# GpSimd takes the low halves of the gate weights and the splitting of each head's output; a head's sink becomes one more column of its scores

## The chip, the cores and the metric

The kernel runs on one NeuronCore of a Trainium2 chip. Five engines work from instruction queues of their own, each in order, and meet only at semaphores: TensorE (PE in the profile, with its weight loads shown apart as PEld), VectorE (DVE), ScalarE (ACT), GpSimd (POOL) and SyncE (SP), which here issues most DMA transfers. The metric is the device time of one execution in microseconds; the median of three runs stands for the kernel.

## The reference

A trunk of two layers over 512 tokens of width 1024, float32. What matters here is the mixer block of each layer:

```python
def mixer_block(h, w_in, b_gate, rel_bias, sinks, w_branch_a, w_branch_b, w_out):
    proj = h @ w_in        # q, k, v of both attentions, and 2048 gate columns
    ya = chunk_relpos_attention(qa, ka, va, rel_bias)      # 8 heads of 64, all earlier chunks
    yb = swa_sink_alibi_attention(qb, kb, vb, sinks)       # 8 heads of 64, 2 chunks back at most
    gates = jax.nn.sigmoid(gate_logits + b_gate)
    merged = gates[:, :, 0] * (ya @ w_branch_a) + gates[:, :, 1] * (yb @ w_branch_b)
    return merged @ w_out

# inside swa_sink_alibi_attention, per head:
    scores = einsum(q, k) * d ** -0.5 + alibi
    m = jnp.maximum(jnp.max(scores, axis=-1, keepdims=True), sink)
    e = jnp.exp(scores - m)
    probs = e / (jnp.sum(e, axis=-1, keepdims=True) + jnp.exp(sink - m))
```

So the sink is a learned number per head that takes part in a row's maximum and in its sum, and has no value vector. Layer 0 ends in a dense SwiGLU, layer 1 in a top-2-of-8 expert SwiGLU.

## The kernel before, in words

Every float32 product is made of three products of rounded halves: a value x is split into hi = round(x) and lo = x - hi, both of a 32-bit type that TensorE takes in one pass, and hi·hi + lo·hi + hi·lo is summed in PSUM. Weights come by DMA in units of 128x1024 into `raw` (4 buffers); ScalarE copies a unit to `w_hi` (`split_hi`), VectorE subtracts to get `w_lo` (`split_lo`, L890), and TensorE multiplies (L1273 to L1275). `w_hi` and `w_lo` have 2 buffers, so unit n+2 is split while unit n+1 is multiplied.

The change lies in the attention stage, which each layer runs through once. It is a loop of 64 steps, called ticks, 4 for each of 16 heads (one for each 128 query rows). Ticks 0 to 31 are heads of kind A, whose rows see 128, 256, 384 and 512 keys; ticks 32 to 63 are heads of kind B, which see 128 or 256 keys. Each engine's program is written out by hand in the order of ticks, and steps of different age are interleaved. In tick t:

- TensorE transposes the probabilities of step t-2 (L1411, after a wait for `probs_ready`), makes the scores of step t (L1421, L1422), multiplies older probabilities by the values (L1439, L1440), and between them works through a quarter of a gate unit (`gate_part`: 6 large products, L1273 to L1275), so that a head has one gate unit beside it. For A heads it also turns the next head's bias (L1384).
- VectorE adds the bias to the scores and takes the negated row maximum in one instruction (L993, in PSUM; in kind B the sink is its starting value), then takes the reciprocal of the sum of step t-1 (L1005) and scales its probabilities by it in SBUF (L1007); in kind B the exponential of the sink is first added to the sum (L1002). Then it makes the low half of the transposed probabilities of step t-2 (L893, `pT_lo`).
- ScalarE copies the high half of the transposed probabilities (L704), and exponentiates the scores (L714); in kind B the sink before them (L712).
- Once per head, in the head's first tick (tick % 4 == 0): ScalarE makes `w_hi` of a gate unit (L595) and then `y_other`, half of an older head's output (L732). VectorE scales a gate's result (L923), makes `w_lo` (L890) and adds the two halves of the output into `y_sum` (L1027), which waits for `y_other`. In the next tick ScalarE copies `y_sum` to its high half (L738) and VectorE subtracts to get the low half (L893, `q_both<-y_sum`). ScalarE also writes the next head's bias tile: out of the turned bias in kind A (L620), as a scaled copy of a distance table in kind B (L623).
- GpSimd has one piece of work per A head: it fetches the next head's bias by DMA (L476) and clears a corner of it (L479). In the 32 ticks of kind B it has none.

After tick 67 the branch products begin (w_a and w_b), which wait for the low half of the last head (`y_lo_ready`).

Of the kernel before, what the change touches and what calls it, by code (L numbers as in the profile page):

```python
# [5 lines left out]
F32 = mybir.dt.float32  # L6
# [8 lines left out]
P = 128  # L15
D = 1024
T = 512
# [46 lines left out]
def build_kernel(nc, xT, g_mix, w_in, b_gate, rel_ext, sinks, w_a, w_b, w_out, g_ffn, w_gu, w_down, w_router,  # L64
                 moe_gu, moe_down, g_ffn_row, g_final_row, out):
    ctx = ExitStack()
    with ctx:
        def sb(name, shape, dt=F32, where=ctx):
            return where.enter_context(nc.sbuf_tensor(name, shape, dt))
# [49 lines left out]
        bias_t = sb("bias_t", [P, 2, T], F32, attn)  # L119
# [6 lines left out]
        nsink = sb("nsink", [P, DEPTH, HEADS], F32, attn)  # L126
# [88 lines left out]
        sink_exp, exp_ready, denom, rcp_ready, probs_ready = sem("sink_exp"), sem("exp_ready"), sem("denom"), sem("rcp_ready"), sem("probs_ready")  # L215
# [219 lines left out]
        def _(pool):  # L435
# [33 lines left out]

            for i in range(DEPTH * HEADS):  # L470
# [117 lines left out]
        def _(act_):  # L588
# [25 lines left out]

            def bias_tile(H, bank):

                layer, hh = H // (2 * HEADS), H % (2 * HEADS)
                if hh < HEADS:
                    A.wait_ge(bias_turned, layer * HEADS + hh + 1)
                    A.activation(bias_t[:, H % 2, 2 * P:], ps[:, bank, 2 * P:], ACT.Identity,  # L620
                                 bias=nfar[:, layer, hh:hh + 1]).then_inc(bias_ready, 1)
                else:
                    A.activation(bias_t[:, H % 2, 2 * P:], alibi[:], ACT.Copy,  # L623
                                 scale=-2.0 ** -(step(TT * hh)["head"] + 1)).then_inc(bias_ready, 1)
# [36 lines left out]
            for layer in range(DEPTH):  # L661
# [33 lines left out]
                for tick in range(STEPS + 6):  # L695
                    if 2 <= tick < STEPS + 2:
                        s, st = layer * STEPS + tick - 2, step(tick - 2)
                        A.wait_ge(pT_ready, s + 1)
                        if st["qb"] == 0 and st["hh"] < 2 * HEADS - 1:
                            bias_tile(layer * 2 * HEADS + st["hh"] + 1, T_BANK + s % 2)  # L700
                        if s >= 4:

                            A.wait_ge(pv_done, s // 2 - 1)
                        A.activation(pT_hi[:, own_blocks(tick - 2), :],  # L704
                                     ps[:, T_BANK + s % 2, 0:st["nk"]].rearrange("p (b c) -> p b c", c=P),
                                     ACT.Copy).then_inc(pT_hi_ready, 1)
                    if tick < STEPS:
                        s, st = layer * STEPS + tick, step(tick)
                        A.wait_ge(nmax_ready, s + 1)
                        c = s % 4  # L710
                        if not st["a"]:
                            A.activation(stat[:, 3, c:c + 1], sink[:, layer, st["head"]:st["head"] + 1], ACT.Exp,  # L712
                                         bias=stat[:, 1, c:c + 1]).then_inc(sink_exp, 1)
                        A.activation(probs[:, s % 2, 0:st["nk"]], ps[:, S_BANK + s % 2, 0:st["nk"]], ACT.Exp, scale=-1.0,  # L714
                                     bias=stat[:, 1, c:c + 1], accum_out=stat[:, 2, c:c + 1]).then_inc(exp_ready, 1)
# [17 lines left out]
                    if tick >= 9 and tick % 4 == 1:  # L733
                        hh = (tick - 9) // 4
                        H = layer * 2 * HEADS + hh
                        r = step(4 * hh)["rows"]
# [149 lines left out]
        def _(V):  # L886
# [38 lines left out]
            def small_consts():  # L925
                V.wait_ge(small_in, 16 * N_SMALL)
                V.tensor_scalar(bg[:], bg[:], 0.5, None, ALU.mult)
                V.tensor_scalar(nfar[:], far[:], -1.0, None, ALU.mult)
                V.tensor_scalar(nsink[:], sink[:], -1.0, None, ALU.mult).then_inc(consts, 1)
# [14 lines left out]
            for layer in range(DEPTH):  # L944
# [39 lines left out]
                for tick in range(STEPS + 6):  # L984
                    if tick < STEPS:
# [4 lines left out]
                        if st["qb"] == 0:  # L990
                            V.wait_ge(bias_ready, H + 1)

                        V.tensor_tensor_reduce(out=sc[:, 0:nk], in0=sc[:, 0:nk], in1=bias_t[:, H % 2, T - nk:], scale=-1.0,  # L993
                                               scalar=-MASKED if st["a"] else nsink[:, layer, st["head"]:st["head"] + 1],
                                               op0=ALU.add, op1=ALU.min, accum_out=stat[:, 1, c:c + 1]).then_inc(nmax_ready, 1)
                    if 1 <= tick < STEPS + 1:
# [3 lines left out]
                        den = stat[:, 2, c:c + 1]  # L1000
                        if not st["a"]:
                            V.tensor_tensor(stat[:, 4, c:c + 1], den, stat[:, 3, c:c + 1], ALU.add).then_inc(denom, 1)  # L1002
                            V.wait_ge(denom, layer * STEPS // 2 + tick - STEPS // 2)
                            den = stat[:, 4, c:c + 1]
                        V.reciprocal(stat[:, 5, c:c + 1], den).then_inc(rcp_ready, 1)  # L1005
# [9 lines left out]
                    if (tick - 4) in GATES_AT:  # L1015
# [4 lines left out]
                        split_lo(n + 2)  # L1020
                    if tick >= 8 and tick % 4 == 0:
# [4 lines left out]
                        V.wait_ge(y_moved, H + 1)  # L1026
                        V.tensor_tensor(y_sum[r:r + HD, :], ps[r:r + HD, O_BANK + hh % 2, :], y_other[r:r + HD, :],  # L1027
                                        ALU.add).then_inc(y_added, 1)
                    if tick >= 9 and tick % 4 == 1:
                        hh = (tick - 9) // 4  # L1030
                        r = step(4 * hh)["rows"]
                        y_hi, y_lo = y_tiles(hh)
                        V.wait_ge(y_hi_ready, layer * 2 * HEADS + hh + 1)
                        lo_of(y_lo[r:r + HD, :], y_sum[r:r + HD, :], y_hi[r:r + HD, :]).then_inc(y_lo_ready, 1)

                for i in range(N_BR // 2):
                    n = n0 + U_BR + 2 * i
                    split_lo(n + 2)
# [227 lines left out]
        def _(E):  # L1266
# [73 lines left out]
            for layer in range(DEPTH):  # L1340
# [46 lines left out]
                for tick in range(STEPS + 4):  # L1387
# [25 lines left out]
                    if tick < STEPS:  # L1413
                        s, st = layer * STEPS + tick, step(tick)
                        k0, nk, qb = st["k0"], st["nk"], st["qb"]
                        if s >= 2:
                            E.wait_ge(exp_ready, s - 1)
                        out = ps[:, S_BANK + s % 2, 0:nk]
# [267 lines left out]
```

## Time and profile before

| | us |
|---|---|
| median of 3 runs (lowest, highest) | 1753.32 (1751.65, 1756.61) |
| span of the profiled execution, first to last instruction | 1750.1 |
| attention loop of layer 0, scores of tick 0 to last products with values | 121 to 296.7 |
| attention loop of layer 1 | 867 to 1041.6 |
| PE busy | 1611.9 (92%) |
| DVE busy | 1097.2 (63%) |
| ACT busy | 884.1 (51%) |
| POOL busy | 99.2 (6%) |

The profile is one execution, and its span leaves out what lies between the start of the measured time and the first instruction. The chain of work that ended last runs 76% over PE, 12% over DVE and 5% over ACT. Matmuls are pipelined and overlap in the records, so PE is never quite at its peak where it is busy.

### The profile page before, as it was taken

The page shows a single profiled execution, that of the slowest core. Times are in us where ns is not written, and L with a number is a line of the kernel's source. Part 1 is how long each engine was busy: PE and PEld are TensorE (multiplying, and loading weights), DVE is VectorE, ACT ScalarE, POOL GpSimd, SP SyncE. Part 2 cuts the span into 40 slices and gives each one's busy share as a digit, 9 for nine tenths or more (in the row PEclk, how much of TensorE's full clock was granted, in tenths as well). Part 3 has the DMA queues.
Part 4 walks back from the last instruction along what each step waited for, and adds up shares of the span by engine and source line. Part 5 has one row for each costly group of instructions (what it writes and reads, how often), then busy time and mean ns, then how long its engine had stood idle before and what let it go on. Part 6 is the DMA issues. An engine that isn't in the chain of part 4 may idle for free.

```text
span 1750.1 us, 22696 instructions
## 1 busy us (share of the span) xinstructions
PE 1611.9 (92%) x7630; PEld 1328.5 (76%) x7631; DVE 1097.2 (63%) x1794; ACT 884.1 (51%) x1422; POOL 99.2 (6%) x148
## 2 busy tenths in 40 slices
PE   8999987999999999999999879969999999999991
PEld 5877765878888878888777658747888888888880
DVE  6647876654444433346478765565656988876665
ACT  5436665243333322234366652445556888875653
POOL 2000000000000000010000000040000001110101
PEclk9999998999999999999999999989999999999995
DMA  7332111223333323343321112155767999997764
GB/s 200 112 96 61 52 49 49 85 84 96 96 97 97 96 81 97 100 134 110 102 61 52 49 48 84 49 229 159 237 200 239 358 364 365 362 338 224 221 221 175
DMA packets 79109, 259.46 MB, mean 148 GB/s; under 512 B 12384, under 2 KB 12384, under 8 KB 78512
## 3 DMA queue, kind: packets, MB, share of 16 engines
q1 hardware_dynamic: 71056, 239.16, 41.6%
q0 software_dynamic: 7968, 19.21, 3.9%
q8 instruction: 48, 0.79, 0.2%
q14 instruction: 37, 0.30, 0.1%
HBM read 244.70 MB, written 9.47 MB: 145 GB/s over the span
## 4 chain that ended last, share of the span: by engine, by line
PE 76%; DVE 12%; ACT 5%; DMA 3%; issue 3%; POOL 0%; SPq 0%; ACTq 0%; POOLq 0%; DVEq 0%; PEldq 0%
PE ps L1273 15%; PE ps L1275 15%; PE ps L1274 15%; PE ps L1553 6%; PE ps L1555 6%; PE ps L1554 6%; PE ps L1551 3%; PE ps L1552 3%; DVE w_lo L890 2%; DVE ps L993 2%; ACT w_hi L595 1%; PE ps L1411 1%; DVE y_sum L1027 1%; DVE m_lo L1175 1%; PE ps L1534 1%
## 5 line engine op out<-in xcount | busy, mean ns | idle before, releaser
L1175 DVE TENSOR_TENSOR m_lo<-m_raw,m_hi 128x1024 fp32r<-128x1024 f32 (+1 forms) x285 | 324.4, 1161 | 110.5 <-ACT m_hi L800 106.7
L800 ACT ACTIVATE m_hi<-m_raw 128x1024 fp32r<-128x1024 f32 (+1 forms) x285 | 284.0, 1010 | 167.8 <-PE ps L1552 132.2
L1273 PE MATMUL ps<-h_hi,w_hi 128*128 128x512 f32 x904 | 361.9, 400 | 5.8 <-DVE h_lo L909 2.9
L595 ACT ACTIVATE w_hi<-raw 128x1024 fp32r<-128x1024 f32 (+1 forms) x169 | 177.1, 1048 | 367.9 <-PE ps L1275 364.6
L1274 PE MATMUL ps<-h_lo,w_hi 128*128 128x512 f32 x904 | 354.5, 392 | 0.0
L1275 PE MATMUL ps<-h_hi,w_lo 128*128 128x512 f32 x904 | 354.4, 392 | 0.0
L890 DVE TENSOR_TENSOR w_lo<-raw,w_hi 128x1024 fp32r<-128x1024 f32 (+1 forms) x169 | 204.7, 1211 | 188.7 <-ACT w_hi L595 186.8
L1275 PEld LDWEIGHTS ps<-h_hi,w_lo 128*128 128x128 f32 x904 | 170.4, 189 | 36.9
L1273 PEld LDWEIGHTS ps<-h_hi,w_hi 128*128 128x128 f32 x904 | 170.9, 189 | 34.3 <-DVE w_lo L890 5.0
L1274 PEld LDWEIGHTS ps<-h_lo,w_hi 128*128 128x128 f32 x904 | 171.0, 189 | 26.7 <-issue 0.7
L1553 PE MATMUL ps<-m_hi,xt_hi 128*128 128x512 f32 (+1 forms) x384 | 145.5, 379 | 6.3 <-DVE m_lo L1175 5.0
L1555 PE MATMUL ps<-m_hi,xt_lo 128*128 128x512 f32 (+1 forms) x384 | 143.5, 374 | 0.0
L1554 PE MATMUL ps<-m_lo,xt_hi 128*128 128x512 f32 (+1 forms) x384 | 143.4, 373 | 0.0
L1553 PEld LDWEIGHTS ps<-m_hi,xt_hi 128*128 128x128 f32 x384 | 72.8, 190 | 19.6 <-DVE m_lo L1175 5.2
L1411 PE MATMUL ps<-ident,probs 128*128 128x128 f32 x272 | 52.8, 280 | 31.9 <-DVE probs L1007 31.7
L714 ACT ACTIVATE probs<-ps,stat 128x256 f32<-128x256 f32 (+3 forms) x128 | 61.2, 478 | 41.3 <-DVE stat L993 40.2
L1554 PEld LDWEIGHTS ps<-m_lo,xt_hi 128*128 128x128 f32 x384 | 72.8, 190 | 10.2
L1555 PEld LDWEIGHTS ps<-m_hi,xt_lo 128*128 128x128 f32 x384 | 72.5, 189 | 10.2
L1411 PEld LDWEIGHTS ps<-ident,probs 128*128 128x128 f32 x272 | 34.7, 140 | 59.2 <-DVE probs L1007 49.3
L1552 PE MATMUL ps<-m_lo,xt_both 128*128 128x512 f32 (+1 forms) x192 | 72.2, 376 | 0.0
L1551 PE MATMUL ps<-m_hi,xt_both 128*128 128x512 f32 (+1 forms) x192 | 72.2, 376 | 0.0
L1553 PE MATMUL ps<-m_hi,at_hi 128*128 128x512 f32 x176 | 70.7, 402 | 1.6 <-PEq L1567 1.6
(234 smaller groups left out, 2759.5 us busy)
## 6 DMA issues: line engine op xcount, KB each, us to landing
m_raw<-moe_g SPq DMA_DIRECT2D x135, 512.0 KB, 5.1
m_raw<-moe_down SPq DMA_DIRECT2D x88, 512.0 KB, 5.2
raw<-w_in SPq DMA_DIRECT2D x68, 512.0 KB, 3.5
m_raw<-moe_g SPq DMA_DIRECT2D x64, 384.0 KB, 3.8
raw<-w_gu SPq DMA_DIRECT2D x44, 512.0 KB, 3.5
raw<-w_out SPq DMA_DIRECT2D x16, 512.0 KB, 3.5
raw<-w_down SPq DMA_DIRECT2D x16, 512.0 KB, 3.6
raw<-w_a SPq DMA_DIRECT2D x8, 512.0 KB, 3.4
```

The lines of the kernel that those rows point to most:

```text
L595: A.activation(split_of(n, 0, cols)[0], raw[:, n % RAW, 0:cols], ACT.Copy).then_inc(hi_ready, 1)
L800: A.activation(m_hi[:, u % M_SPL, 0:cols], m_raw[:, u % M_RAW, 0:cols], ACT.Copy).then_inc(m_hi_ready, 1)
L890: V.tensor_tensor(lo, raw[:, n % RAW, 0:cols], hi.bitcast(F32), ALU.subtract).then_inc(lo_ready, 1)
L1175: V.tensor_tensor(m_lo[:, u % M_SPL, 0:cols], m_raw[:, u % M_RAW, 0:cols], m_hi[:, u % M_SPL, 0:cols].bitcast(F32), ALU.subtract).then_inc ...
L1273: E.matmul(ps[:, bank, :], wh, hi, start=first, stop=False)
L1274: E.matmul(ps[:, bank, :], wh, lo, start=False, stop=False)
L1275: return E.matmul(ps[:, bank, :], wl, hi, start=False, stop=final)
L1551: E.matmul(out, both[:, x, :], wh, start=start, stop=False)
L1552: return E.matmul(out, both[:, x, :], wl, start=False, stop=stop)
L1553: E.matmul(out, hi[:, x, :], wh, start=start, stop=False)
L1554: E.matmul(out, hi[:, x, :], wl, start=False, stop=False)
L1555: return E.matmul(out, lo[:, x, :], wh, start=False, stop=stop)
```

## The change

GpSimd does three things more in the attention stage: `w_lo` of the 16 gate-stage units of each layer (`gate_lo`), both halves of each head's output (`head_split`), and the bias tile of each B head (`distance_tile`), with the head's sink in a 513th column. VectorE and ScalarE lose these. In kind B the sink is now one more column of the scores: VectorE's instruction takes one more PSUM column, which is zero, adds the bias tile with the sink in it, and writes its sum not to PSUM but to `probs` in SBUF; ScalarE exponentiates there, in place, one column more, and its running sum holds the sink's part already. The separate exponential, the addition to the sum and the negated sinks are gone. TensorE's wait before the scores of step t is for the maximum of step t-2 in kind B, not for its exponential.

The new functions of GpSimd, the order in which it calls them, and what goes from VectorE and ScalarE:

```diff
+            def gate_lo(layer, g):
+                n = MIX_START[layer] + U_GATE + g + 2
+                hi, lo = split_of(n, 0, UNIT)
+                pool.wait_ge(hi_ready, n + 1)
+                pool.wait_ge(lo_ready, n)
+                pool.tensor_tensor(lo, raw[:, n % RAW, :], hi.bitcast(F32), ALU.subtract).then_inc(lo_ready, 1)
+                pool.wait_ge(lo_ready, n + 1)
+            def distance_tile(layer, hh):
...
+                pool.wait_ge(nmax_ready, TT * (H - 1))
+                pool.tensor_scalar(bias_t[:, H % 2, 2 * P:T], alibi[:], -2.0 ** -(head + 1), None, ALU.mult)
+                pool.wait_ge(bias_ready, H)
+                pool.tensor_copy(bias_t[:, H % 2, T:T + 1], sink[:, layer, head:head + 1]).then_inc(bias_ready, 1)
+            def head_split(layer, hh):
...
+                pool.wait_ge(y_added, H + 1)
+                pool.tensor_copy(y_hi[r:r + HD, :], y_sum[r:r + HD, :]).then_inc(y_hi_ready, 1)
+                pool.wait_ge(y_hi_ready, H + 1)
+                pool.tensor_tensor(y_lo[r:r + HD, :], y_sum[r:r + HD, :], y_hi[r:r + HD, :].bitcast(F32),
+                                   ALU.subtract).then_inc(y_lo_ready, 1)
+                pool.wait_ge(y_lo_ready, H + 1)
             for i in range(DEPTH * HEADS):
...
+                pool.wait_ge(bias_masked, i + 1)
+                if i % HEADS >= 2:
+                    gate_lo(i // HEADS, i % HEADS - 2)
+                if i % HEADS >= 3:
+                    head_split(i // HEADS, i % HEADS - 3)
+                if i % HEADS == HEADS - 1:
+                    for j in range(HEADS - 2, 2 * HEADS):
+                        gate_lo(i // HEADS, j)
+                        head_split(i // HEADS, j - 1)
+                        if j + 2 < 2 * HEADS:
+                            distance_tile(i // HEADS, j + 2)
+                    head_split(i // HEADS, 2 * HEADS - 1)
...
-                        if not st["a"]:
-                            A.activation(stat[:, 3, c:c + 1], sink[:, layer, st["head"]:st["head"] + 1], ACT.Exp,
-                                         bias=stat[:, 1, c:c + 1]).then_inc(sink_exp, 1)
+                            A.activation(probs[:, s % 2, 0:st["nk"] + 1], probs[:, s % 2, 0:st["nk"] + 1], ACT.Exp, scale=-1.0,
+                                         bias=stat[:, 1, c:c + 1], accum_out=stat[:, 2, c:c + 1]).then_inc(exp_ready, 1)
...
-                        A.wait_ge(y_added, H + 1)
-                        A.activation(y_tiles(hh)[0][r:r + HD, :], y_sum[r:r + HD, :], ACT.Copy).then_inc(y_hi_ready, 1)
...
+                            if tick < STEPS // 2 + 2:
+                                V.memset(sc[:, 2 * P:2 * P + 1], 0.0).then_inc(sink_column, 1)
+                                V.wait_ge(sink_column, 2 * layer + tick - STEPS // 2 + 1)
+                            V.wait_ge(pT_ready, s - 1)
+                            V.tensor_tensor_reduce(out=probs[:, s % 2, 0:nk + 1], in0=sc[:, 2 * P - nk:2 * P + 1],
+                                                   in1=bias_t[:, H % 2, T - nk:T + 1], scale=-1.0, scalar=-MASKED,
+                                                   op0=ALU.add, op1=ALU.min, accum_out=stat[:, 1, c:c + 1]).then_inc(nmax_ready, 1)
...
-                            V.tensor_tensor(stat[:, 4, c:c + 1], den, stat[:, 3, c:c + 1], ALU.add).then_inc(denom, 1)
...
-                        split_lo(n + 2)
...
-                        lo_of(y_lo[r:r + HD, :], y_sum[r:r + HD, :], y_hi[r:r + HD, :]).then_inc(y_lo_ready, 1)
```

On VectorE, in the middle of a B head of the program before, from the last row of the head's first tick to the first rows of the third (`w_lo` is the gate weights' low half, `q_both<-y_sum` the head's):

```order
L923 TENSOR_TENSOR gates<-ps,rms_inv 128x512
L890 TENSOR_TENSOR w_lo<-raw,w_hi 128x1024
L1027 TENSOR_TENSOR y_sum<-ps,y_other 64x512
L993 ISA ps,stat<-ps,bias_t,nsink 128x256
L993 ISA stat 128x1
L1002 TENSOR_TENSOR stat<-stat 128x1
L1005 RECIPROCAL stat<-stat 128x1
L1007 TENSOR_SCALAR probs<-probs,stat 128x128
L893 TENSOR_TENSOR pT_lo<-ps,pT_hi 128x2x128
L893 TENSOR_TENSOR q_both<-y_sum,q_both 64x512
L993 ISA ps,stat<-ps,bias_t,nsink 128x256
```

The same place in the changed program (L1034 is now the addition with the maximum, L1043 the scaling):

```order
L956 TENSOR_TENSOR gates<-ps,rms_inv 128x512
L1064 TENSOR_TENSOR y_sum<-ps,y_other 64x512
L1034 ISA probs,stat<-ps,bias_t 128x257
L1034 ISA stat 128x1
L1041 RECIPROCAL stat<-stat 128x1
L1043 TENSOR_SCALAR probs<-probs,stat 128x128
L926 TENSOR_TENSOR pT_lo<-ps,pT_hi 128x2x128
L1034 ISA probs,stat<-ps,bias_t 128x257
```

Three instructions are gone from between the gate's scaling and the next step's scores, two of them large. On GpSimd, for the last A heads before, where it goes from bias to bias:

```order
L479 MEMSET norm 64x64
L476 DMA norm<-rel_ext 128x256
L479 MEMSET norm 64x64
L476 DMA norm<-rel_ext 128x256
```

and in the changed program, through the last of these biases into the first of the B heads:

```order
L507 DMA norm<-rel_ext 128x256
L510 MEMSET norm 64x64
L475 TENSOR_TENSOR w_lo<-raw,w_hi 128x1024
L495 CAST q_both<-y_sum 64x512
L497 TENSOR_TENSOR q_both<-y_sum,q_both 64x512
L475 TENSOR_TENSOR w_lo<-raw,w_hi 128x1024
L495 CAST q_both<-y_sum 64x512
L497 TENSOR_TENSOR q_both<-y_sum,q_both 64x512
L485 TENSOR_SCALAR bias_t<-alibi 128x256
L487 COPY bias_t<-sink 128x1
```

Each head now gives GpSimd a weight unit and an output in two instructions, and in kind B a bias tile, all in one queue.

## Rows read from the trace of the kernel before

**Rows 1.** Windows, kind A and kind B ticks: us, busy per engine, PEclk, DMA, GB/s.
```profile
121.20:205.20 84.00, 79.36 (x432) 65.09 (x430) 61.91 (x182) 54.88 (x130) 5.03 (x14) 0.98 0.21 60
205.20:289.10 83.90, 69.03 (x385) 54.58 (x383) 66.66 (x217) 55.99 (x163) 0.00 (x0) 1.00 0.17 51
```

**Rows 2.** Timeline of a B head's long tick: start us, us, engine, line, instruction [idle before].
```profile
238.62 1.05 ACT L595 ACTIVATE w_hi<-raw 128x1024 fp32r<-128x1024 f32 x1
...
239.70 0.59 ACT L732 ACTIVATE y_other<-ps 64x512 f32<-64x512 f32 x1
239.71 1.23 DVE L890 TENSOR_TENSOR w_lo<-raw,w_hi 128x1024 fp32r<-128x1024 f32 x1
...
240.96 0.69 DVE L1027 TENSOR_TENSOR y_sum<-ps,y_other 64x512 f32<-64x512 f32 x1
...
242.59 0.29 DVE L1007 TENSOR_SCALAR probs<-probs,stat 128x128 f32<-128x128 f32 x1
...
242.93 0.33 PE L1411 MATMUL ps<-ident,probs 128*128 128x128 f32 x1 [1.59 <-DVE probs L1007]
```

**Rows 3.** Timeline, TensorE's last score product (L1422) of each tick, two B heads.
```profile
226.87 0.28 PE L1422 MATMUL ps<-kb_lo,q_both 128*128 128x128 f32 x1
...
237.32 0.28 PE L1422 MATMUL ps<-kb_lo,q_both 128*128 128x128 f32 x1
239.44 0.28 PE L1422 MATMUL ps<-kb_lo,q_both 128*128 128x256 f32 x1
243.22 0.29 PE L1422 MATMUL ps<-kb_lo,q_both 128*128 128x256 f32 x1
...
248.42 0.28 PE L1422 MATMUL ps<-kb_lo,q_both 128*128 128x128 f32 x1
```

**Rows 4.** Groups by form: count | busy us, mean ns of one | idle before, releaser.
```profile
L893 DVE TENSOR_TENSOR q_both<-y_sum,q_both 64x512 fp32r<-64x512 f32 x32 | 22.0, 686 | 12.6 <-ACT q_both L738 12.6
L738 ACT ACTIVATE q_both<-y_sum 64x512 fp32r<-64x512 f32 x32 | 20.0, 624 | 3.6 <-DVE y_sum L1027 3.2
L712 ACT ACTIVATE stat<-sink,stat 128x1 f32<-128x1 f32 x64 | 18.8, 294 | 44.8 <-DVE stat L993 44.5
L1007 DVE TENSOR_SCALAR probs<-probs,stat 128x512 f32<-128x512 f32 x16 | 7.8, 487 | 0.7
```

**Rows 5.** Groups of GpSimd by form.
```profile
L516 POOL TENSOR_TENSOR h_rows<-h_rows,g_row 128x1024 f32<-128x1024 f32 x4 | 9.4, 2354 | 8.3 <-ACT h_rows L631 8.2
L479 POOL MEMSET norm<- 64x64 f32 x16 | 2.5, 158 | 45.1 <-DMA norm<-rel_ext 45.1
L519 POOL MEMSET m_act<- 64x512 f32 x1 | 0.5, 517 | 0.0
```

**Rows 6.** Timeline of the kernel's last stage, where VectorE and GpSimd work beside each other.
```profile
1735.06 1.28 DVE L1254 SCALAR_TENSOR_TENSOR x_rows<-h_rows,r,x_rows 128x1024 f32<-128x1024 f32 x1
1736.06 2.49 POOL L584 TENSOR_TENSOR x_rows<-x_rows,g_row 128x1024 f32<-128x1024 f32 x1 [17.02 <-ACT x_rows L882]
1736.33 3.30 DVE L1251 SCALAR_TENSOR_TENSOR x_rows<-h_rows,r,x_rows 128x1024 f32<-128x1024 f32 x1
```

**Rows 7.** Timeline, a clearing by GpSimd that begins beside a scaling.
```profile
129.92 0.42 DVE L1007 TENSOR_SCALAR probs<-probs,stat 128x384 f32<-128x384 f32 x1
130.08 0.35 POOL L479 MEMSET norm<- 64x64 f32 x1 [2.69 <-DMA norm<-rel_ext]
```

**Rows 8.** Timeline of two A heads: weight split and the next tick's scaling.
```profile
152.46 1.05 ACT L595 ACTIVATE w_hi<-raw 128x1024 fp32r<-128x1024 f32 x1
...
156.22 0.29 DVE L1007 TENSOR_SCALAR probs<-probs,stat 128x128 f32<-128x128 f32 x1
...
163.38 1.05 ACT L595 ACTIVATE w_hi<-raw 128x1024 fp32r<-128x1024 f32 x1
...
166.78 0.28 DVE L1007 TENSOR_SCALAR probs<-probs,stat 128x128 f32<-128x128 f32 x1
```

**Rows 9.** Timeline, the first branch product after the attention loop of layer 0.
```profile
299.53 0.79 PE L1273 MATMUL ps<-q_both,w_hi 128*128 128x512 f32 x1 [2.79 <-DVE q_both L893]
```

More of the change, by code:

```diff
@@ L468, in double_keys @@
                         pool.dma_start(lo[other, :], lo[own, :]).then_inc(k_doubled, 16)
+            def gate_lo(layer, g):
[6 more added lines that the diff above has]
+            def distance_tile(layer, hh):
+                H = layer * 2 * HEADS + hh
+                head = step(TT * hh)["head"]
+                if hh == HEADS:
+                    pool.wait_ge(consts, 4)
+                pool.wait_ge(nmax_ready, TT * (H - 1))
[3 more added lines that the diff above has]
+            def head_split(layer, hh):
+                H = layer * 2 * HEADS + hh
+                r = step(4 * hh)["rows"]
+                y_hi, y_lo = y_tiles(hh)
+                pool.wait_ge(y_added, H + 1)
[4 more added lines that the diff above has]
+                pool.wait_ge(y_lo_ready, H + 1)
             for i in range(DEPTH * HEADS):
@@ L617, in bias_tile @@
                 layer, hh = H // (2 * HEADS), H % (2 * HEADS)
[L618 to L624, printed above, removed]
+                A.wait_ge(bias_turned, layer * HEADS + hh + 1)
+                A.activation(bias_t[:, H % 2, 2 * P:T], ps[:, bank, 2 * P:], ACT.Identity,
+                             bias=nfar[:, layer, hh:hh + 1]).then_inc(bias_ready, 1)
             def x_copy(t):
@@ L927, in small_consts @@
                 V.tensor_scalar(bg[:], bg[:], 0.5, None, ALU.mult)
-                V.tensor_scalar(nfar[:], far[:], -1.0, None, ALU.mult)
-                V.tensor_scalar(nsink[:], sink[:], -1.0, None, ALU.mult).then_inc(consts, 1)
+                V.tensor_scalar(nfar[:], far[:], -1.0, None, ALU.mult).then_inc(consts, 1)
                 V.wait_ge(consts, 3)
@@ L999, in _ @@
                         V.wait_ge(exp_ready, s + 1)
-                        den = stat[:, 2, c:c + 1]
-                        if not st["a"]:
-                            V.tensor_tensor(stat[:, 4, c:c + 1], den, stat[:, 3, c:c + 1], ALU.add).then_inc(denom, 1)
-                            V.wait_ge(denom, layer * STEPS // 2 + tick - STEPS // 2)
-                            den = stat[:, 4, c:c + 1]
-                        V.reciprocal(stat[:, 5, c:c + 1], den).then_inc(rcp_ready, 1)
+                        V.reciprocal(stat[:, 5, c:c + 1], stat[:, 2, c:c + 1]).then_inc(rcp_ready, 1)
                         V.wait_ge(rcp_ready, s + 1)
@@ L1026, in _ @@
                         V.wait_ge(y_moved, H + 1)
+                        if hh >= 2:
+                            V.wait_ge(y_lo_ready, H - 1)
                         V.tensor_tensor(y_sum[r:r + HD, :], ps[r:r + HD, O_BANK + hh % 2, :], y_other[r:r + HD, :],
                                         ALU.add).then_inc(y_added, 1)
[L1029 to L1033, printed above, removed]
-                        lo_of(y_lo[r:r + HD, :], y_sum[r:r + HD, :], y_hi[r:r + HD, :]).then_inc(y_lo_ready, 1)
                 for i in range(N_BR // 2):
                     n = n0 + U_BR + 2 * i
+                    if i == 0:
+                        V.wait_ge(lo_ready, n + 2)
                     split_lo(n + 2)
@@ L1415, in _ @@
                         k0, nk, qb = st["k0"], st["nk"], st["qb"]
-                        if s >= 2:
+                        if tick >= 2 and not step(tick - 2)["a"]:
+                            E.wait_ge(nmax_ready, s - 1)
+                        elif s >= 2:
                             E.wait_ge(exp_ready, s - 1)
-                        out = ps[:, S_BANK + s % 2, 0:nk]
+                        out = ps[:, S_BANK + s % 2, 0:nk] if st["a"] else ps[:, S_BANK + s % 2, 2 * P - nk:2 * P]
                         q = q_both[:, st["hh"], qb * P:(qb + 1) * P]
```

25 lines of the change are left out of this document (12 added, 13 removed).

## The prediction

> **What bounds the kernel now.** I read the page's busy shares first: PE is at 92% over the span, so only the stages in which it waits have anything to give. The windows over the attention loop of layer 0 say which these are: in the A ticks PE is busy 79.36 of 84.00 us, in the B ticks 69.03 of 83.90 [rows 1]. So 14.9 us are open in a layer's B ticks and 4.6 in its A ticks, 39 us in both layers, and no edit here can bring more than that. VectorE is busy 66.66 us and ScalarE 55.99 us of the B window, neither full, so the idle time comes of order, not of load.
>
> The timeline of a B head shows the order [rows 2]. In the head's first tick ScalarE makes `w_hi` (238.62 to 239.67) and then `y_other` (to 240.29). VectorE makes `w_lo` meanwhile (to 240.94), adds `y_sum` (to 241.65), and only then takes the next scores; their predecessors' scaling starts at 242.59, and TensorE, idle for 1.59 us, starts its transposes at 242.93. The distances of the last score products give the same: 2.12, 3.78 and then 5.20 us for two ticks, 11.10 in all; the head before took 10.45 [rows 3]. Heads of the two lengths alternate, so a mean B head takes 10.78 us. A tick in which PE doesn't wait lasts about 2.2 us (69.03 us of work over 32 ticks is 2.16 [rows 1]), so the second of these four ticks is long by 1.6, and the last two together by about 0.8.
>
> **The change, part by part.**
>
> *Leaving VectorE.* Per head, `w_lo` of 1.23 us [rows 2] and the head's low half of 0.69 us [rows 4]; per B tick the small addition before the reciprocal. *Leaving ScalarE.* Per head, the high half of 0.62 us, and per B tick the sink's exponential of 0.29 us [rows 4]. The last one matters beyond its size: it stands before `w_hi`, so `w_hi` of a B head starts about 0.20 us earlier (I leave 0.09 for what the longer exponential out of SBUF may cost). Were GpSimd free of all side effects, that would be the whole of it.
>
> *Coming to GpSimd.* A subtraction of 128x1024 takes it 2.35 us, by its other instructions of that size [rows 5]. The head's low half is 64x512, so half of that, 1.17 us. The copy to the high half is not in the trace: between 0.52 us (a clearing of 64x512 [rows 5]) and 1.17 us (the subtraction). I take 0.65, near the clearing and near ScalarE's 0.62 for the same copy [rows 4]. The bias tile of 128x256 lies between 0.16 us (a small clearing [rows 5]) and 0.6 us (a quarter of 2.35). Together 4.2 to 5.3 us a head of 9.5 or more: GpSimd keeps up, and nothing that it makes is needed before the second next head. Its bias fetches for A heads are done before the head's `w_lo` is wanted, since they start 6 ticks ahead.
>
> *What GpSimd does to VectorE.* This is the term that decides. The trace shows twice that the two exclude each other. At the end, a VectorE instruction that takes 1.28 us when alone takes 3.30 when it starts at 1736.33 beside a GpSimd multiplication (1736.06 to 1738.55): it ends at 1739.63, so it began its work at 1738.35, 0.20 us before GpSimd's recorded end [rows 6]. And a clearing on GpSimd, 0.16 us in the mean [rows 5], took 0.35 when it began inside a scaling by VectorE, 129.92 to 130.34 [rows 7]. So the scaling (L1007) can be held up by GpSimd. The scaling's form points the same way: 0.29 us for 128 columns [rows 2] and 0.487 for 512 [rows 4] are 0.51 ns a column, where `w_lo` takes 1.23 us for 1024, 1.2 ns a column. It runs at double pace, SBUF to SBUF. The Trainium skill has the rule (SBUF — State Buffer, "Who interferes with whom"): a VectorE instruction in a 2-port mode, or with two SBUF inputs against a GpSimd instruction that reads SBUF, excludes GpSimd, and the second to start is fully blocked; "VectorE: DVE Perf Modes" (section "Mode 2×_2P") names float32 `tensor_scalar` in SBUF as one of the 2-port kind. The trace agrees in both directions, with the 3.30 and the 0.35 us above. The other VectorE work of the loop reads one operand from PSUM; I take it to run on beside GpSimd.
>
> So in the head's second tick the scaling starts no earlier than GpSimd's release: start of `w_hi` + 1.05 + a hand-over of 0.08 + 2.35 - 0.20 = start + 3.28 us.
> - Odd B heads: 238.42 + 3.28 = 241.70 in place of 242.59, 0.89 us earlier [rows 2]. The tick of 3.78 becomes 2.89. The last two ticks lose VectorE's and ScalarE's split, and become 2.20 + 2.24 = 4.44 if GpSimd's own split doesn't take its place: the copy starts after the scaling, and copy and subtraction release VectorE 0.65 + 0.10 + 1.17 - 0.20 = 1.7 us later, while the next scaling, itself of 0.35 us, must start within about 1.8 us for TensorE not to wait in a tick of 2.2. It just fits. Sum 2.12 + 2.89 + 4.44 = 9.45 in place of 11.10.
> - Even B heads end at the same 9.45, since what differed between the two was VectorE's queue; 1.00 us less than 10.45 [rows 3].
> - Mean 1.32 us a head, 8 heads: **10.6 us a layer**.
> - A heads with the whole load (heads 2 to 7): the scaling comes 3.76 and 3.40 us after the start of `w_hi` in the two kinds [rows 8]; after, 3.28. That is 0.48 and 0.12 us, three heads each, 1.8 us. Head 1 has `w_lo` but no output yet, so its scaling was early; it loses about 0.3. Their other ticks are bound by PE. **1.5 us a layer.**
>
> *After the loop.* The first branch product waits 2.79 us for the last head's low half [rows 9], behind copy and subtraction of 0.62 + 0.69. On GpSimd these take 0.65 + 1.17 (at most 1.17 + 1.17), 0.5 to 1.0 more; but `w_lo` no longer stands before the last transposed half on VectorE, which gives back 0.4 of the 0.65 by which it outlasts `y_other` [rows 2]. Cost 0.1 to 0.6 a layer; 0.3.
>
> *The sink's column.* Four tiny clearings with a wait, two per layer, at most 0.3 us each by the sink's exponential, which is as small [rows 4]: 0.6 in all. Writing to SBUF adds a wait for transposes that TensorE has issued before the scores, so it costs nothing; one more column costs about 1 ns.
>
> *Sum.* 2 x (10.6 + 1.5 - 0.3) - 0.6 = 23.0 us. The span goes from 1750.1 to 1727; the median stands 3.2 above the span, so **1730 us**.
>
> **The rivals.**
> 1. *VectorE's scaling is not held up.* Then it follows `y_sum`, and that follows `y_other`: 240.29 - 0.20 + 0.69 + the 0.94 from the end of `y_sum` to the scaling - 0.2 for the addition = 241.52, 1.07 earlier than now [rows 2], 0.18 better than above. In A heads the gain is 0.68 and 0.56 in place of 0.48 and 0.12. A layer gains 12.0 + 3.7: 1753.3 - 31.4 + 1.2 = 1723. Against it stand rows 6 and 7; for it, that both show other instructions or the other direction.
> 2. *GpSimd's copy is slow, at 1.17 us.* Then the second scaling starts 0.5 later than it may, in each B head, and about 0.2 in A heads: 2 x (4.0 + 1.2) less, and 0.5 a layer after the loop: 1741.
> 3. *GpSimd's subtraction takes longer with this output type; the kernel gets slower.* The place is the scaling behind `w_lo`, once per head, in 15 heads of a layer. Each microsecond over 2.35 costs 15 a layer, so the gain of about 11.5 is gone at 3.1 us, and beyond that the kernel loses. No row shows GpSimd writing the rounded type of `w_lo`; one of its multiplications of this size took 2.49 us though nothing held it up at its start [rows 6], the others 2.35 [rows 5]. At 3.6 us: 1730 + 2 x 15 x 1.25 = 1767.
> 4. *The idle time stays where it is*, since `y_sum` still waits behind `w_hi` and `y_other` on ScalarE. That holds for the start of the tick, and is in the sum; the 0.65 us from the end of `y_other` to the end of `w_lo` and the split in the next tick do go. A gain under 0.3% (5 us) needs both this and part of 2 or 3.
>
> **How the numbers follow.** 0.3% is about what a measurement of this kernel can tell from no change. Forecast with the hold-up as worked out: 0.48, around 1730. Rival 1: 0.17, at 1723. Rival 2: 0.18, at 1741. Rival 3: 0.12, mostly above 1759. Rival 4: 0.05, near 1750. Rivals 1 and 2 are faster too, so faster 0.83, same 0.05, slower 0.12. The range of 8 in 10 reaches from under rival 1 (all of PE's idle time in the loop but a quarter, 1753 - 34 = 1719) to above rival 2 with a subtraction of 2.5 us on top (1741 + 4.5 = 1746).
>
> **What would show it.** In the profile after, `w_lo` on GpSimd should last 2.35 us and begin within 0.1 us of the end of `w_hi`. Of the 128 scalings, those in a head's second tick should be recorded long, or start at the end of GpSimd's `w_lo`; if none is over 0.5 us, rival 1 holds. The four tick lengths of a B head should be near 2.1, 2.9, 2.2, 2.2, the same in odd and even heads. PE's busy time in the B window should stay 69 us in a window of about 73. The A window should shrink by 1 to 2 us only. A GpSimd copy near 1.2 us with a third tick near 2.6 would be rival 2. The forecast is wrong if the second tick doesn't shrink, or if TensorE's wait after the loop grows by more than 1 us.

## The result, and the profile after

The changed kernel takes 1782.65 us (median of 4 runs, 1780.45 to 1783.67), the kernel before beside it 1752.49. The ratio is 1.0171, 95% interval 1.0154 to 1.0187: 30 us slower, where 23 us faster was forecast.

The attention loop did what the forecast says. Windows of layer 0 in the changed kernel, A ticks and B ticks, which answer to [rows 1]:

```profile
121.30:204.10 82.80, 79.09 (x434) 65.17 (x433) 54.27 (x169) 51.68 (x124) 34.06 (x35) 0.99 0.21 59
204.10:277.70 73.60, 68.31 (x384) 54.70 (x383) 52.71 (x173) 46.51 (x118) 41.33 (x38) 1.00 0.19 58
```

The A ticks take 82.8 us for 84.0, the B ticks 73.6 for 83.9. The last score products of one B head, as in [rows 3]:

```profile
232.44 0.28 PE L1456 MATMUL ps<-kb_lo,q_both 128*128 128x128 f32 x1
...
234.58 0.28 PE L1456 MATMUL ps<-kb_lo,q_both 128*128 128x256 f32 x1
...
237.44 0.28 PE L1456 MATMUL ps<-kb_lo,q_both 128*128 128x256 f32 x1
...
239.67 0.29 PE L1456 MATMUL ps<-kb_lo,q_both 128*128 128x256 f32 x1
...
241.91 0.28 PE L1456 MATMUL ps<-kb_lo,q_both 128*128 128x128 f32 x1
```

Ticks of 2.14, 2.86, 2.23 and 2.24, together 9.47; forecast were 2.12, 2.89 and 4.44, together 9.45. The same head's timeline shows how the second tick is set, in place of [rows 2]:

```profile
233.49 1.04 ACT L638 ACTIVATE w_hi<-raw 128x1024 fp32r<-128x1024 f32 x1
...
234.62 2.39 POOL L475 TENSOR_TENSOR w_lo<-raw,w_hi 128x1024 fp32r<-128x1024 f32 x1 [3.85 <-ACT w_hi L638]
...
235.19 0.69 DVE L1064 TENSOR_TENSOR y_sum<-ps,y_other 64x512 f32<-64x512 f32 x1 [0.74 <-ACT y_other L772]
...
236.46 0.64 DVE L1043 TENSOR_SCALAR probs<-probs,stat 128x128 f32<-128x128 f32 x1
...
237.08 0.61 POOL L495 CAST q_both<-y_sum 64x512 fp32r<-64x512 f32 x1
...
237.77 1.29 POOL L497 TENSOR_TENSOR q_both<-y_sum,q_both 64x512 fp32r<-64x512 f32 x1
...
238.30 0.92 DVE L1043 TENSOR_SCALAR probs<-probs,stat 128x256 f32<-128x256 f32 x1
```

The first scaling is recorded with 0.64 us where its form takes 0.29 [rows 2]. It ends at 237.10, so its work began at 236.81, 0.20 us before the recorded end of GpSimd's `w_lo` (237.01): the same 0.20 as in [rows 6]. The next one (0.92 us) begins beside the head's low half on GpSimd (L497, to 239.06) and ends 0.16 us behind it. Of the 128 scalings 48 are recorded with more than 0.5 us. GpSimd's prices, beside [rows 5]:

```profile
L475 POOL TENSOR_TENSOR w_lo<-raw,w_hi 128x1024 fp32r<-128x1024 f32 x32 | 76.3, 2386 | 114.9 <-ACT w_hi L638 64.1 <-issue 50.7
L497 POOL TENSOR_TENSOR q_both<-y_sum,q_both 64x512 fp32r<-64x512 f32 x32 | 41.2, 1288 | 2.6
...
L495 POOL CAST q_both<-y_sum 64x512 fp32r<-64x512 f32 x32 | 19.4, 607 | 2.1
L485 POOL TENSOR_SCALAR bias_t<-alibi 128x256 f32<-128x256 f32 x16 | 13.7, 853 | 1.4
```

After the loop of layer 0 TensorE waits 3.94 us for GpSimd's last low half, 1.15 us more than in [rows 9] (in layer 1 3.75 us for 2.79, 0.96 more):

```profile
287.75 0.80 PE L1305 MATMUL ps<-q_both,w_hi 128*128 128x512 f32 x1 [3.94 <-POOL q_both L497]
```

**Where the time went.** It went into the expert stage, over 100 us behind the last attention loop, where the change touches nothing. The windows from the head of the first expert pass to ScalarE's last activation of the last pass show it, the kernel before first, then the changed one:

```profile
1184.80:1715.10 530.30, 519.36 (x2500) 442.66 (x2500) 387.44 (x411) 359.62 (x436) 38.73 (x33) 0.99 0.80 273
```
```profile
1163.50:1745.90 582.40, 531.73 (x2500) 449.89 (x2500) 387.71 (x412) 358.76 (x436) 37.45 (x33) 0.95 0.74 249
```

The changed kernel enters it 21.3 us earlier (1163.5 for 1184.8) and takes 52.1 us more for it. TensorE is idle for 50.7 us where it was for 10.9, and its granted clock is 0.95 for 0.99, so that its work lasts 12.4 us longer too. The waits of that stage in the changed kernel (who waits for whom: us in total, times, longest):

```profile
ACT L855 <- issue: 61.0, 8, 10.4
PEld ps L1587 <- DVE m_lo L1207: 48.4, 12, 10.6
PE ps L1587 <- DVE m_lo L1207: 43.7, 11, 10.2
```

and the same ones before:

```profile
PE ps L1553 <- DVE m_lo L1175: 5.0, 8, 2.7
...
ACT L822 <- issue: 0.6, 1, 0.6
```

L855 (L822 before) is ScalarE's first instruction in each of the 8 passes of the expert loop, a dummy activation that loads a table. ScalarE's timeline between two passes, changed kernel:

```profile
1330.64 1.00 ACT L886 ACTIVATE y_stage<-ps 128x1024 f32<-128x1024 f32 x1
1331.67 1.02 ACT L889 ACTIVATE m_other<-ps 64x1024 f32<-64x1024 f32 x1
1342.79 1.28 ACT L855 ACT_TABLE_LOAD   x1 [10.10 <-issue]
```

and before:

```profile
1353.77 1.03 ACT L856 ACTIVATE m_other<-ps 64x1024 f32<-64x1024 f32 x1
1354.81 1.28 ACT L822 ACT_TABLE_LOAD   x1
```

"issue" means that the engine waited for nothing the profile shows. Of the changed kernel's eight waits the one at the first pass, which the loop enters from above, is 0.61 us; the seven behind a branch back to the loop's head are 5.74 to 10.43 us. ScalarE makes `m_hi` of the experts' weights, and without it VectorE can't make `m_lo`. TensorE works off the units in store (`m_hi` and `m_lo` have five buffers), and is then idle for 10.15 us in this pass and restarts more slowly (a product recorded with 0.79 us for 0.39; the granted clock is 0.50, half of full speed, from 1346.5 to 1349.0):

```profile
1336.01 0.39 PE L1589 MATMUL ps<-m_hi,xt_lo 128*128 128x512 f32 x1
1346.55 0.79 PE L1587 MATMUL ps<-m_hi,xt_hi 128*128 128x512 f32 x1 [10.15 <-DVE m_lo L1207]
```

The DMA part of the page names what else changed, the instruction fetches of one queue; the changed kernel's line, then the line before:

```profile
q14 instruction: 71, 0.58, 0.1%
```
```profile
q14 instruction: 37, 0.30, 0.1%
```

These packets are of 8 KB. What was added falls into the expert stage. The same line for the two windows above, changed kernel and before, and for 1332.7 to 1342.8, ScalarE's idle time in the changed kernel's timeline:

```profile
q14 instruction: 42, 0.34, 0.2%
```
```profile
q14 instruction: 7, 0.06, 0.0%
```
```profile
q14 instruction: 4, 0.03, 0.9%
```

The trace also keeps ScalarE's register and branch instructions, which the page leaves out. In this idle time ScalarE branches back to the head of the loop at 1333.7 and its next instruction comes 6.03 us later; it then branches to one of the loop's two variants, and the next instruction comes 2.35 us later. In the loop of the kernel before, no branch of ScalarE is followed by more than 0.43 us of nothing.

By the trace, ScalarE runs 1197 instructions before the loop, where it ran 1293: 96 fewer (112 activations taken out, 16 semaphore waits that now stand alone). So the theory to test was that the loop had moved in ScalarE's program against the pieces in which instructions are fetched. The Trainium skill knows the effect ("Runtime: NRT & Kernel Launch", section "Instruction fetch mechanics"): instruction memory holds two blocks of 16 KiB, and a taken branch whose target is outside them forces a fetch before the engine can go on. The trace agrees in kind, with the 6.03 and 2.35 us behind two branches; the size of a block is a matter for the experiments.

### The profile page after: what moved, and what is told of

Its sections match the earlier page's. It is cut to its first block, busy times and chain, and to the rows that moved or that the text cites. A ratio compares the mean times of both kernels' runs of the same rounds, so it can differ in the third digit from the quotient of the medians.

```text
span 1780.2 us, 22778 instructions
## 1 busy us (share of the span) xinstructions
PE 1623.2 (91%) x7630; PEld 1336.7 (75%) x7631; DVE 1047.9 (59%) x1669; ACT 854.3 (48%) x1310; POOL 252.4 (14%) x276
## 3 DMA queue, kind: packets, MB, share of 16 engines
HBM read 244.70 MB, written 9.47 MB: 143 GB/s over the span
## 4 chain that ended last, share of the span: by engine, by line
PE 77%; DVE 7%; issue 7%; ACT 5%; DMA 2%; POOL 1%; ACTq 0%; SPq 0%; POOLq 0%; PEldq 0%; DVEq 0%
PE ps L1305 15%; PE ps L1306 15%; PE ps L1307 15%; PE ps L1587 6%; PE ps L1588 6%; PE ps L1589 6%; PE ps L1585 3%; PE ps L1586 3%; ACT w_hi L638 2%; PE ps L1443 1%; DVE probs L1043 1%; PE ps L1568 1%; ACT y_other L772 1%; PE ps L1456 1%; PE ps L1597 1%
## 5 line engine op out<-in xcount | busy, mean ns | idle before, releaser
L923 DVE TENSOR_TENSOR w_lo<-raw,w_hi 128x1024 fp32r<-128x1024 f32 x137 | 165.8, 1210 | 192.3 <-ACT w_hi L638 192.1
L1587 PE MATMUL ps<-m_hi,xt_hi 128*128 128x512 f32 (+1 forms) x384 | 150.8, 393 | 46.0 <-DVE m_lo L1207 43.7
L1588 PE MATMUL ps<-m_lo,xt_hi 128*128 128x512 f32 (+1 forms) x384 | 147.7, 385 | 0.0
L1589 PE MATMUL ps<-m_hi,xt_lo 128*128 128x512 f32 (+1 forms) x384 | 147.2, 383 | 0.0
L584 POOL DMA_INDIRECT xg<-h_dram,lists x20 | 26.7, 1335 | 514.7 <-PE ps L1568 367.8
L475 POOL TENSOR_TENSOR w_lo<-raw,w_hi 128x1024 fp32r<-128x1024 f32 x32 | 76.3, 2386 | 114.9 <-ACT w_hi L638 64.1
L507 POOL DMA_DIRECT2D norm<-rel_ext x16 | 9.2, 578 | 557.7 <-PE ps L1332 494.3
L1043 DVE TENSOR_SCALAR probs<-probs,stat 128x256 f32<-128x256 f32 (+3 forms) x128 | 69.3, 542 | 5.0
```

The costliest lines, as they stand in the source:

```text
L923: V.tensor_tensor(lo, raw[:, n % RAW, 0:cols], hi.bitcast(F32), ALU.subtract).then_inc(lo_ready, 1)
L1043: V.tensor_scalar(t[:, 0:nk], t[:, 0:nk], stat[:, 5, c:c + 1], None, ALU.mult).then_inc(probs_ready, 1)
L1587: E.matmul(out, hi[:, x, :], wh, start=start, stop=False)
L1588: E.matmul(out, hi[:, x, :], wl, start=False, stop=False)
L1589: return E.matmul(out, lo[:, x, :], wh, start=False, stop=stop)
```

## The experiments

All kernels "with increments" have that many increments of an unused semaphore at one place, where ScalarE waits for the first transposed rows:

```diff
             for u in range(M_SPL):
                 expert_hi(16, u)
+            for _ in range(96):
+                A.sem_inc(padding, 1)
             turned_x(0, 0)
```

### The place of ScalarE's loop

**96 increments in the changed kernel.**

> The changed kernel with 96 tiny semaphore increments added to ScalarE's program ahead of the expert loop (between the first five weight copies and the first transposed rows, where ScalarE waits over 11 us). Nothing else differs. Theory, place of the loop in ScalarE's program: the changed kernel ran 96 ScalarE instructions fewer before the loop, which moved the loop against the 8 KB pieces in which its instructions are fetched; the increments put it back. Expected: no fetches in the loop, no idle time at the loop's head (61 us in 8 passes now), attention as in the changed kernel, so 1730 to 1734 us. Rival, the work moved to GpSimd or the new place of data slows the expert stage: unchanged, 1780 to 1785 us.

Measured: 1730.83 us (1727.45 to 1733.62), ratio to before 0.988 (0.9862 to 0.9898). ScalarE's waits for issue at the loop's heads are 0.6 us, the expert stage takes its 530.3 us again:

```profile
1164.10:1694.40 530.30, 519.14 (x2500) 442.48 (x2500) 387.10 (x412) 359.46 (x436) 39.04 (x33) 0.99 0.80 273
```

The queue's line reads 37 packets again, and the ticks of the loop are those of the changed kernel (9.44 to 9.46 in B heads, but for the first of a layer). Ninety-six instructions that do nothing for the result make the kernel 52 us faster.

**32 increments in the kernel before.**

> The kernel before with 32 such increments at the same place. 32 more and 96 fewer put the loop at the same place within 128 instructions (8 KB). Theory: the expert stage takes what it takes in the changed kernel, 50 us more, so about 1803 us, with 6 to 8 us idle at the head of most passes on ScalarE and some 35 more instruction fetches. Rival (the moved work is the cause): unchanged, 1750 to 1757 us.

Measured: 1803.2 us (1800.5 to 1806.32), ratio 1.0289 (1.0272 to 1.0306), 72 packets, and

```profile
ACT L825 <- issue: 61.4, 8, 11.2
```

No part of the change is in this kernel, and it has the whole loss, 51.8 us. That leaves nothing for the rivals, the work moved to GpSimd or a new place of the data.

**128 increments in the changed kernel.**

> The changed kernel with 128 increments ahead of ScalarE's expert loop, 32 more than in the kernel that took 1731 us. Theory, place against pieces of 128 instructions (8 KB): a shift by a whole piece changes nothing against the changed kernel, so the stall is back: 1780 to 1785 us, about 61 us idle at the heads of the passes. Rival, the increments helped since they add time or distance before the loop: stays at 1729 to 1735 us.

Measured: 1777.66 us in one run, 56.9 us idle at the loop's heads, 73 packets. More instructions than the good kernel has, and slow again.

**48 increments.**

> The changed kernel with 48 increments ahead of ScalarE's expert loop. Theory: what counts is how many pieces of 128 instructions the loop touches. It is 296 instructions long (5 at its head, 149 in one branch, 136 in the other, 6 around), which touch 4 pieces from 40 of 128 starting places and 3 from the other 88. The starting place of the changed kernel is one of the 40, so one moved by 48 isn't: 1729 to 1735 us, no idle time at the loop's head. Rival, only the exact place of the kernel before is good: 1777 to 1785 us.

Measured: 1732.68 us in one run, 0.6 us idle, 36 packets.

**16 increments.**

> The changed kernel with 16 increments. By the same count the starting place moved by 16 may still be among the 40 or past them; either 1729 to 1735 or 1777 to 1785 us, and nothing between if a piece is the unit. Rival, the cost grows with the distance: something between, near 1765.

Measured: 1780.72 us in one run, 49.9 us idle, 71 packets. So the loop stalls at places 0, 16 and 128 and not at 48 and 96 (counted from the changed kernel's), with nothing between. This is what a unit of 128 instructions gives, if a packet of 8 KB holds so many; five places do not measure the unit's size closer, and the last three are single runs, told apart by 45 us. The Trainium skill's block of 256 instructions would put 128 half a block away, where a loop of 296 should not stall if it stalls at 0; for this engine the measurement decides against that figure. The mechanism, a fetch behind a taken branch, fits all five places and the gaps behind the branches in the trace. How many pieces the engine holds is not shown: a loop of 296 instructions is longer than two pieces of 128, and it doesn't stall at places 48 and 96.

### The parts of the change

**`w_lo` back on VectorE.** Edit: `gate_lo` is no longer called, `split_lo(n + 2)` is back behind the gate's scaling; 96 increments.

> The changed kernel with the 96 increments, and the gate weights' low half back on VectorE; the heads' splits, the bias tiles and the sink's column stay changed. Theory, the exclusion of scaling and GpSimd costs little here since ScalarE's w_hi and y_other come before: VectorE then makes w_lo until 0.65 us after y_other, so a B head's second tick is 3.3 to 3.5 in place of 2.86 and a head 9.9 to 10.1; the A heads 10.5 to 10.7. About 7 to 10 us slower than with w_lo on GpSimd (1738 to 1743). Rival, GpSimd's w_lo holds VectorE up for more than VectorE's own takes: the same or faster, 1725 to 1732.

Measured: 1734.14 us (1733.22 to 1736.39), ratio 0.9898 (0.9882 to 0.9915), which overlaps that with `w_lo` on GpSimd (0.9862 to 0.9898). The second ticks of B heads are 2.91 and 3.15, their sums 9.36 and 9.60, on average 9.48; with GpSimd 9.46. I expected 9.9 to 10.1. Moving `w_lo` bought next to nothing in B heads; in A heads 2 to 7 it bought 0.1 and 0.4 (10.67 and 10.93 against 10.56, in head 7 10.46 against 10.07), of which head 1 gives back 0.6 (9.98 to 10.56; I had said 0.3).

**The sink's column and the bias tiles alone.** Edit: the heads' splits back on ScalarE and VectorE as well; 64 increments, so that ScalarE runs 1293 instructions before its loop, as before.

> The changed kernel with w_lo and the heads' splits back on VectorE and ScalarE, so that only the sink's column and the bias tiles on GpSimd stay changed; 64 increments (ScalarE's program then as long before the loop as in the kernel before). Theory from the time line: in B ticks ScalarE starts w_hi 0.2 us earlier and VectorE loses the addition of 0.15 plus its wait, so the second tick goes from 3.42 and 3.77 to 3.2 and 3.6, the third from 2.66 and 2.96 to 2.4 and 2.7; a B head 10.3 in place of 10.78; A heads as before. 4 us a layer, so 1742 to 1746 us. Rival, the sink's column carries most of the gain: 1737 or less.

Measured: 1739.02 us (1738.24 to 1742.62), ratio 0.9932 (0.9909 to 0.9955). B heads take 9.66 and 10.16, 0.87 less than before in the mean. The rival came close: this part gives 12 of the 21 us. One reason is in the groups by form: in B ticks the addition with the maximum is 0.06 us shorter. Two rows of the kernel before, B heads and A heads, then the changed kernel's B heads:

```profile
L993 DVE CUSTOM_DVE_ANT_0 ps<-ps,bias_t,nsink 128x256 f32<-128x256 f32 x48 | 23.4, 487 | 9.7 <-PE ps L1422 9.2
L993 DVE CUSTOM_DVE_ANT_0 ps<-ps,bias_t 128x256 f32<-128x256 f32 x16 | 6.8, 423 | 3.3 <-PE ps L1422 3.1
```
```profile
L1034 DVE CUSTOM_DVE_ANT_0 probs<-ps,bias_t 128x257 f32<-128x257 f32 x48 | 20.4, 424 | 14.6 <-PE ps L1456 14.2
```

The second row writes to PSUM and takes 0.423 us, as the last does that writes to SBUF. So the 0.06 us does not come from where the sum goes: it goes away with the starting value read from the tile `nsink`, for which there is a constant now, as in A heads. How the 0.87 us a head divides among this, the addition of 0.15 us and the exponential of 0.29 us that are gone, and TensorE's wait, now for the maximum, was not measured.

### GpSimd against the scaling

**A quarter of `w_lo`.** Edit: `lo[:, 0:256]` and likewise for the inputs; the other 768 columns of each gate-stage unit's low half are left out, while TensorE makes all its products as before.

> The changed kernel with the 96 increments, in which GpSimd makes only the first 256 of 1024 columns of each gate unit's low half (the rest of those products is left out). Theory, the scaling waits for GpSimd's release only by a little: a B head's second tick falls from 2.86 to 2.6 to 2.75 (then ScalarE's y_other sets it), an A head's from 3.25 to 2.7 to 3.0, and no scaling of the second tick is recorded longer than 0.5 us for w_lo's sake. Rival, the tick is not set by w_lo on GpSimd at all: ticks unchanged at 2.86 and 3.25.

Measured: 1718.75 us in one run. B heads: second tick 2.45 to 2.50, third 2.08, sum 8.90 to 8.98; A heads: 2.81 and 2.96. No scaling is recorded with more than 0.49 us. The theory's direction, and more of it than I expected: with three quarters of `w_lo` out of the way the second tick loses 0.37 in B.

**`w_lo` in four parts.** Edit:

```diff
-                pool.tensor_tensor(lo, raw[:, n % RAW, :], hi.bitcast(F32), ALU.subtract).then_inc(lo_ready, 1)
+                for q in range(4):
+                    c = slice(q * UNIT // 4, (q + 1) * UNIT // 4)
+                    pool.tensor_tensor(lo[:, c], raw[:, n % RAW, c], hi[:, c].bitcast(F32), ALU.subtract).then_inc(
+                        lo_ready if q == 4 - 1 else lo_part, 1)
+                    if q < 4 - 1:
+                        lo_parts[0] += 1
+                        pool.wait_ge(lo_part, lo_parts[0])
```

> The changed kernel with the 96 increments and GpSimd's w_lo in four instructions of 256 columns, each after the one before has ended, the same work in all. Theory, the exclusion is for one instruction: the scaling slips in after the part that runs, so it waits 0.5 us at most; second ticks fall from 2.86 to 2.5 to 2.7 (B) and from 3.25 to 2.85 to 3.0 (A), as with a quarter of the work; 1719 to 1724 us. Rival, the parts follow each other too closely for VectorE to get in, or cost more in all: 1729 to 1736 us.

Measured: 1731.38 us (1727.07 to 1732.65), ratio 0.9876 (0.9851 to 0.99): no gain. The timeline of a B head shows both why and that the scaling does slip in:

```profile
234.54 3.17 POOL L480 TENSOR_TENSOR w_lo<-raw,w_hi 128x256 fp32r<-128x256 f32 x4 [2.92 <-ACT w_hi L647]
...
235.10 0.70 DVE L1075 TENSOR_TENSOR y_sum<-ps,y_other 64x512 f32<-64x512 f32 x1 [0.73 <-ACT y_other L781]
...
236.38 0.61 DVE L1054 TENSOR_SCALAR probs<-probs,stat 128x128 f32<-128x128 f32 x1
```

The scaling ends at 236.99 while the four parts last until 237.71. By the trace the third part ends at 236.91 and the fourth begins at 236.98: it ran between these two. But it can't start before `y_sum`, which waits for ScalarE's `y_other`, and the four parts take 3.2 us in all for the 2.4 us of the one. The second tick is 2.82, the head 9.29; A heads get 0.1 longer.

**Four parts, and `y_other` ahead of `w_hi`.** Edit: ScalarE's block for `y_other` moved in front of the block for the gate unit.

> As the kernel with w_lo in four parts, and ScalarE makes y_other ahead of w_hi instead of behind it. Theory, with the hold-up short the second tick is set by w_hi and y_other on ScalarE: y_sum comes 1.05 us earlier, TensorE no longer waits in any tick, second ticks 2.1 to 2.3 (B) and 2.5 to 2.6 (A), a B head 8.7 to 8.9: 1711 to 1717 us. Rival, w_lo then runs beside the scalings of the second and third tick and holds them up: no better than with four parts alone.

Measured: **1712.16 us** (1710.07 to 1715.95), ratio 0.9768 (0.9747 to 0.979), the fastest here. Its windows of layer 0, A and B ticks:

```profile
119.40:197.00 77.60, 77.60 (x433) 65.46 (x431) 51.36 (x169) 51.28 (x123) 38.27 (x56) 0.98 0.22 64
197.00:266.40 69.40, 68.39 (x384) 54.83 (x384) 52.89 (x173) 46.10 (x117) 44.02 (x61) 1.00 0.18 54
```

TensorE is busy nearly all through; the two windows together are 147.0 us where the kernel before takes 167.9 [rows 1]. The second ticks of A heads are 2.45 to 2.52, B heads take 8.89 to 9.13, a little over the expected 8.7 to 8.9 (their last tick is now 2.5: a scaling is recorded with 1.25 us beside GpSimd's split).

**`y_other` ahead of `w_hi`, `w_lo` whole.**

> The changed kernel with the 96 increments and y_other ahead of w_hi on ScalarE, w_lo on GpSimd in one instruction. Theory, the scaling of the second tick waits for GpSimd's release, and w_hi now ends 0.6 us later: second ticks 3.4 to 3.5 (B) and 3.8 to 3.9 (A), so 15 to 18 us more than 1731: 1744 to 1750 us. Rival, ScalarE's order alone made the gain of the kernel with four parts: 1712 to 1718 us.

Measured: 1749.42 us (1748.47 to 1752.42), ratio 0.999 (0.9981 to 1.0): the gain of the loop is gone. Second ticks 3.46 and 3.59 in B.

```profile
241.37 2.36 POOL L476 TENSOR_TENSOR w_lo<-raw,w_hi 128x1024 fp32r<-128x1024 f32 x1 [4.60 <-ACT w_hi L639]
...
241.75 2.06 DVE L1046 TENSOR_SCALAR probs<-probs,stat 128x128 f32<-128x128 f32 x1
...
243.86 0.33 PE L1446 MATMUL ps<-ident,probs 128*128 128x128 f32 x1 [1.40 <-DVE probs L1046]
```

A scaling of 0.29 us is recorded with 2.06: it is recorded from 0.4 us after GpSimd began, and ends at 243.81, 0.08 after GpSimd's recorded end. The same move of `y_other` costs 19 us with `w_lo` in one piece and gains 19 with it in four: the new order on ScalarE and the cut into four gain only together.

## Why the prediction was wrong

The step that failed is the last of the sum: "The span goes from 1750.1 to 1727". It carries a gain of the attention loop unchanged to the end, and takes the rest of the program as it was. Measured, the changed kernel is 21.3 us ahead at the first expert pass, and then loses 52. Each part of the change was priced by what it does where it stands; what 96 fewer instructions of ScalarE do to the program behind them stands in the sum at nothing, without a reason. The change does not touch the expert loop's instructions, only their place. The kernel before with 32 idle instructions has the loss without the change, and the changed kernel with 96 takes 1730.83 us. That this is so near the forecast's 1730 is in part luck: the gain there is 20.6 us for 23.0, and the kernel before took 1751.4 beside it, not 1753.3.

The other steps:

- *What bounds the loop*: right. PE's idle time in a layer's B ticks went from 14.9 to 5.3 us.
- *The hold-up of the scaling by GpSimd*, start of `w_hi` + 3.28 us: right. In the head shown the release is at 233.49 + 3.32 = 236.81. Second, third and fourth ticks 2.86, 2.23, 2.24 for 2.89, 2.20, 2.24; odd and even heads alike, as forecast, but for the first B head of a layer (9.7 in all). B ticks 10.3 us a layer for 10.6, A ticks 1.2 for 1.5.
- *What it costs*: I set it at 0.18 us a head against no hold-up at all (rival 1). The quarter of `w_lo`, which still leaves GpSimd 0.74 us of it, says at least 0.37 in the second tick and 0.15 in the third. Rival 1 is refuted as a description (48 scalings are over 0.5 us), and its price for the hold-up was too small.
- *GpSimd's prices*: 2.39 for 2.35, 1.29 for 1.17, 0.61 for 0.65; the bias tile 0.85, over the bound of 0.6. Rivals 2 and 3, which needed longer ones, did not occur.
- *After the loop*: mis-sized. TensorE's wait grew by 1.15 us in layer 0, past the 1 us that I named as a sign of error, and by 0.96 in layer 1, so by 0.85 and 0.66 us over the 0.3 in the sum.
- *Which part gains*: not resolved in the forecast, and my expectations for it were wrong. The sink's column carries 12 us, the heads' splits about 5 (1739.0 to 1734.1), `w_lo` about 3 (to 1730.8, within the intervals). B heads are as short with `w_lo` on VectorE (9.48 for 9.46), so the right tick lengths do not show that its move was worth what the forecast gives it.
- *Rival 3* stood on the right side of the result for the wrong reason; no rival had the mechanism.
- *The range*: its lower end is said to leave a quarter of PE's idle time in the loop; 34 of 39 us leave an eighth.

How ScalarE's fetching works inside is not settled. That the 34 added packets are ScalarE's is inferred: they come and go with its idle time in all 13 kernels (71 to 73 packets in the four that stall, 36 to 38 in the other nine). Why a pass pays 3.6 to 11.2 us in these four was not tried.

## What to carry to other kernels

Here the speed of a loop of 296 instructions with branches depends on where it begins in its engine's program, and an edit ahead of it, which touches nothing in it, lost 3%. The same may hold for other long loops. After an edit ahead of one, look at the idle time with releaser "issue" at the loop's first instruction and at the count of instruction packets before judging the edit; and compare two versions only with equal places, which some idle instructions ahead of the loop can give. Work given to GpSimd was not free here, since a VectorE scaling on the path waited for GpSimd's whole instruction; cut into four instructions, and with the order on ScalarE fitted to it, the same work gained 19 us more.

## What the hardware showed that I had not expected

- The changed kernel with 0, 16 or 128 increments ahead of ScalarE's loop takes 1777.7 to 1782.7 us, with 48 or 96 1730.8 to 1732.7. In the first three up to 6.03 us pass between a branch of ScalarE and its next instruction.
- GpSimd's subtraction of 128x256 takes 0.73 to 0.74 us, more than a quarter of the 2.39 us for 128x1024; an estimate from the two is a fixed part of 0.2 us.
- VectorE's addition with the maximum takes 0.487 us with a starting value from a tile, and 0.423 with a constant; whether it writes to PSUM (0.423) or, with one column more, to SBUF (0.424) makes no difference.
- The scaling's record includes its wait for GpSimd: the same form reads 0.29 us alone and 0.64 or 2.06 us behind GpSimd, and both times its last 0.29 us begin 0.20 us (0.21 in the second) before GpSimd's recorded end.
